# Running sums of a chunked scan: one product per head on the full array, against rows made once and spread by products over 32 rows

## The reference, cut to what matters

```python
A = adt.reshape(bsz, nc, SSD_CHUNK, SSD_GROUPS, SSD_HEADS_PER_GROUP).transpose(0, 3, 4, 1, 2)
A_cs = jnp.cumsum(A, axis=-1)
seg = A_cs[..., :, None] - A_cs[..., None, :]
Lmat = jnp.exp(jnp.where(tril, seg, -jnp.inf))
CB = jnp.einsum('bclgn,bcsgn->bcgls', Cc, Bc)
y_diag = jnp.einsum('bcgls,bgecls,bcsgep->bclgep', CB, Lmat, X)
```

## Time and profile before

| what | value |
|---|---|
| time, median of 3 runs | 3142.99 us (3139.17 to 3147.56) |
| span of the profiled execution | 3139.9 us |
| TensorE busy | 2900.7 us, 92% |
| VectorE busy | 1044.5 us, 33% |
| ScalarE busy | 569.5 us, 18% |
| mean granted TensorE clock | 0.966 |

### The profile page before, as it was taken

The page is one execution under the profiler, slowest core; times in us unless marked ns, Lnnn a source line. Parts: engine busy times, 40 slices in busy tenths (PEclk is TensorE's granted clock), DMA queues, the critical chain, the costliest instruction groups (busy, mean ns, idle before and its releaser), DMA issues. The chain is left out here.

```text
span 3139.9 us, 34204 instructions
## 1 busy us (share of the span) xinstructions
PE 2900.7 (92%) x14022; PEld 1723.2 (55%) x14022; DVE 1044.5 (33%) x2724; ACT 569.5 (18%) x1272; POOL 205.5 (7%) x369
## 2 busy tenths in 40 slices
PE   7999999999999999999999799999959997898985
PEld 4577647854567647865576455454424564343332
DVE  3444423413443523522464422121131253111112
ACT  1232311101221412102253100000010241000001
POOL 0000230000000000000000000000022020000001
PEclk9999999999999999999999899999979998999998
DMA  5357476343346437342311299999963215999996
GB/s 203 134 168 259 153 222 241 112 147 136 134 141 249 176 110 260 127 164 64 107 55 36 100 415 426 426 426 428 427 255 89 85 50 233 427 429 427 428 427 279
DMA packets 183286, 720.05 MB, mean 229 GB/s; under 512 B 16049, under 2 KB 25233, under 8 KB 158033
## 3 DMA queue, kind: packets, MB, share of 16 engines
q1 hardware_dynamic: 163600, 667.51, 54.3%
q0 software_dynamic: 19232, 50.24, 5.0%
q10 hardware_dynamic: 288, 0.01, 0.0%
HBM read 694.02 MB, written 25.53 MB: 229 GB/s over the span
## 5 line engine op out<-in xcount | busy, mean ns | idle before, releaser
L2429 PE MATMUL bank<-wslot,xgT 128*64 128x512 f32 x1040 | 488.2, 626 | 71.7 <-DMA wslot<-in_moe_w_up 68.3
L2430 PE MATMUL bank<-wslot,xgT 128*64 128x512 f32 x1040 | 488.7, 627 | 0.0
L554 PE MATMUL bank<-h1T,wslot 128*128 128x256 f32 x2176 | 476.4, 381 | 2.3 <-issue 2.2
L554 PEld LDWEIGHTS bank<-h1T,wslot 128*128 128x128 f32 x2176 | 413.1, 191 | 61.8 <-issue 6.0
L2429 PEld LDWEIGHTS bank<-wslot,xgT 128*64 128x64 f32 x1040 | 144.4, 143 | 336.5 <-issue 336.5
L2446 DVE TENSOR_TENSOR hid<-gs,bank 64x512 f32<-64x512 f32 x65 | 67.8, 1043 | 519.2 <-ACT gs L2440 519.2
L2484 PE MATMUL bank<-wslot,aT 128*64 128x512 f32 x1040 | 230.4, 595 | 1.5 <-DVE aT L643 1.5
L2404 PEld LDWEIGHTS bank<-sel,hT 128*128 128x128 f32 x1600 | 186.8, 197 | 39.5 <-issue 25.1
L2404 PE MATMUL bank<-sel,hT 128*128 128x128 f32 x1600 | 193.0, 282 | 14.1 <-DVE sel L2383 14.1
L2430 PEld LDWEIGHTS bank<-wslot,xgT 128*64 128x64 f32 x1040 | 144.4, 143 | 34.3 <-issue 34.3
L2484 PEld LDWEIGHTS bank<-wslot,aT 128*64 128x64 f32 x1040 | 73.0, 137 | 135.0 <-issue 131.3
(11 more groups left out here) (388 smaller groups left out, 3526.3 us busy)
## 6 DMA issues: line engine op xcount, KB each, us to landing
wslot<-in_moe_w_gate SPq DMA_DIRECT2D x65, 2048.0 KB, 16.1
wslot<-in_moe_w_up SPq DMA_DIRECT2D x65, 2048.0 KB, 12.3
wslot<-in_moe_w_down SPq DMA_DIRECT2D x65, 2048.0 KB, 13.2
wslot<-in_w_in SPq DMA_DIRECT2D x36, 2048.0 KB, 8.9
wslot<-in_w_ada SPq DMA_DIRECT2D x24, 2048.0 KB, 8.1
wslot<-in_ffn_w_up SPq DMA_DIRECT2D x20, 2048.0 KB, 9.1
y_rows<-yo POOLq DMA_DIRECT2D x130, 128.0 KB, 7.7
wslot<-in_w_proj_ssd SPq DMA_DIRECT2D x8, 2048.0 KB, 9.3
```

The lines of the kernel that those rows point to most:

```text
L554: ins = pe.matmul(b.t[:, 0:width], w[:, k, j * P:(j + 1) * P], xT(k), start=(k == 0), stop=(k == kc - 1))
L2429: pe.matmul(bk.t[other, :], xt.t[:, k, mine], wg[:, k, :], start=(k == 0), stop=(k == KD - 1))
L2430: ins = pe.matmul(bk.t[mine, :], xt.t[:, k, mine], wu[:, k, :], start=(k == 0), stop=(k == KD - 1))
```

## The change

`sums` makes the running sums a second time, as rows: four products with `ADT` as weights (32 columns, one column group of the array each) and `upto` as moving operand, so that the 32 heads stand on partitions 0 to 31, and again on 32 to 63, 64 to 95 and 96 to 127. VectorE copies them to a new tile `sumT`. In `chunk`, the eight products contract over 32 rows: weights one column of the identity broadcast to 128 columns, moving operand a block of 32 rows of `sumT`. Four products that follow each other lie on four row groups and write four banks, two heads a bank. All four banks are taken at once and waited for at once, VectorE adds the mask in four operations of 128x256, and one mark behind all eight products releases the first of these. The loan of a bank keeps the order of the turn: `lend` takes the bank whose turn it is, `back` puts it at the end of the list after bringing `n` below the length.

```diff
+    def lend(self):
+        at = self.n % len(self.bufs)
+        b = self.bufs.pop(at)
+        self.n = at
+        return b
+
+    def back(self, b):
+        self.n %= len(self.bufs)
+        self.bufs.append(b)
...
-        held = K.banks.bufs.pop()
+        held = K.banks.lend()
...
+        sumT = K.sb("sumT", [P, TT, P], ctx=ctx)
...
                 pe.matmul(b.t[:, 0:SHEADS], K.c("upto"), d(ADT), start=True, stop=True)
+                for i in range(P // SHEADS):
+                    pe.matmul(b.t[SHEADS * i:SHEADS * (i + 1), P:2 * P], d(ADT), K.c("upto"), start=True, stop=True)
...
+                K.dve.mark(v.tensor_copy(sumT[:, t, :], b.t[:, P:2 * P]).then_inc(K.dve.sem, 1))
...
-        K.banks.bufs.append(held)
+        K.banks.back(held)
...
-                for q, hs in enumerate(heads):
-                    bq = K.banks.next()
...
-                        for due in K.due(pe, *small, *bq.free):
...
-                            ins = pe.matmul(bq.t[:, i * P:(i + 1) * P],
-                                            dts[:, t, ADT, h:h + 1].broadcast_to([P, P]), K.c("upto"),
-                                            start=True, stop=True)
+                rows4 = P // SHEADS
+                bqs, exps = [K.banks.next() for _ in range(rows4)], []
...
+                    for due in K.due(pe, *small, *[m for bq in bqs for m in bq.free]):
+                        pe.wait_ge(*due)
+                    for j in range(2):
+                        for i, bq in enumerate(bqs):
+                            at, h = SHEADS * i, HPG * g + 2 * i + j
+                            ins = pe.matmul(bq.t[:, j * P:(j + 1) * P],
+                                            K.ident[at:at + SHEADS, at + h:at + h + 1].broadcast_to([SHEADS, P]),
+                                            sumT[at:at + SHEADS, t, :], start=True, stop=True)
+                    K.mp = K.pe.mark(ins.then_inc(K.pe.sem, 1))
+                spread = K.mp
+                for i, bq in enumerate(bqs):
...
-                            dc.t[:, 4 * q:4 * q + 4, :], bq.t[:, :].rearrange("p (h l) -> p h l", h=4),
-                            K.c("segmask").unsqueeze(1).broadcast_to([P, 4, P]), ALU.add).then_inc(K.dve.sem, 1))
+                            dc.t[:, 2 * i:2 * i + 2, :], bq.t[:, 0:2 * P].rearrange("p (h l) -> p h l", h=2),
+                            K.c("segmask").unsqueeze(1).broadcast_to([P, 2, P]), ALU.add).then_inc(K.dve.sem, 1))
```

More of the change, by code:

```diff
@@ L1374, in chunk @@
                 dc = decay.next()
-                heads = [[HPG * g + 4 * q + i for i in range(4)] for q in range(HPG // 4)]
-                exps = []
-                for q, hs in enumerate(heads):
-                    bq = K.banks.next()
-                    @block.tensor
-                    def _(pe):
-                        for due in K.due(pe, *small, *bq.free):
-                            pe.wait_ge(*due)
-                        for i, h in enumerate(hs):
-                            ins = pe.matmul(bq.t[:, i * P:(i + 1) * P],
-                                            dts[:, t, ADT, h:h + 1].broadcast_to([P, P]), K.c("upto"),
-                                            start=True, stop=True)
-                        K.mp = K.pe.mark(ins.then_inc(K.pe.sem, 1))
+                rows4 = P // SHEADS
@@ new lines, in chunk, with _ @@
+                bqs, exps = [K.banks.next() for _ in range(rows4)], []
+                @block.tensor
+                def _(pe):
+                    for due in K.due(pe, *small, *[m for bq in bqs for m in bq.free]):
[7 more added lines that the diff above has]
+                    K.mp = K.pe.mark(ins.then_inc(K.pe.sem, 1))
@@ L1390, in _ @@
+                spread = K.mp
+                for i, bq in enumerate(bqs):
                     @block.vector
                     def _(v):
-                        for due in K.due(v, K.mp, *dc.free):
+                        for due in K.due(v, spread, *dc.free):
                             v.wait_ge(*due)
                         K.mv = K.dve.mark(v.tensor_tensor(
-                            dc.t[:, 4 * q:4 * q + 4, :], bq.t[:, :].rearrange("p (h l) -> p h l", h=4),
-                            K.c("segmask").unsqueeze(1).broadcast_to([P, 4, P]), ALU.add).then_inc(K.dve.sem, 1))
+                            dc.t[:, 2 * i:2 * i + 2, :], bq.t[:, 0:2 * P].rearrange("p (h l) -> p h l", h=2),
+                            K.c("segmask").unsqueeze(1).broadcast_to([P, 2, P]), ALU.add).then_inc(K.dve.sem, 1))
@@ L1402, in _ @@
                             act.wait_ge(*due)
-                        for i, h in enumerate(hs):
-                            K.ml = K.act.mark(act.activation(dc.t[:, 4 * q + i, :], dc.t[:, 4 * q + i, :], ACT.Exp,
+                        for j in range(2):
+                            h = HPG * g + 2 * i + j
+                            K.ml = K.act.mark(act.activation(dc.t[:, 2 * i + j, :], dc.t[:, 2 * i + j, :], ACT.Exp,
                                                              bias=dts[:, t, NCS, h:h + 1]).then_inc(K.act.sem, 1))
@@ L1407, in chunk @@
                 yield
-                for q, hs in enumerate(heads):
+                for q in range(2):
                     @block.vector
                     def _(v):
-                        for due in K.due(v, exps[q], cm):
+                        for due in K.due(v, exps[2 * q + 1], cm):
                             v.wait_ge(*due)
@@ L2627, in route @@
         late, dif, incl = self.kept
-        logits = K.banks.bufs.pop()
+        logits = K.banks.lend()
         logits_free = logits.free
@@ L2741, in route @@
         chosen = K.mv
-        K.banks.bufs.append(logits)
+        K.banks.back(logits)
         b = K.banks.next()
```

## The result

The changed kernel takes 3160.54 us (median of seven runs, 3146.25 to 3162.06); the kernel before, on the same chip, 3141.41 us (seven runs, 3139.17 to 3147.56). These two also ran at a higher mean granted clock, 0.967 and 0.966, where the other five have 0.962 to 0.965. The forecast was 3144.0 us with a range from 3135 to 3151. The profiled execution took 3161.46 us for a span of 3159.6, 19.7 us more than the span in the earlier trace rows.

A forecast was written before the change was run, and what follows sets the result against it. TensorE was taken to set the scan's pace, with VectorE, which empties the banks, behind. Bank order -6.0, sums +1.0, banks +0.9 and clock +5.1 gave +1.0 us on the median 3142.99: 3144.0 us, range 3135 to 3151.

The forecast's parts named there:

- Spreading on four row groups: Scan: a chunk's spreading products take 0.75 instead of 1.79 us, 16.6 us less in all if nothing else holds TensorE.
- The banks: Scan: second chunks wait about 2 us for four banks, released by VectorE's mask; no gain from faster products, +0.9 us.
- The clock: Behind eight new scan waits of about 2.0 us: three falls to half clock at 1.7 us each, +5.1 us.
- The sums: In `sums`: four more products of 32 columns a chunk, 0.5 us in a layer, +1.0 us.
- The order of the banks: Layer 2 before its sums: the held bank comes seventh or eighth, so the 6.30 us wait shrinks, -6.0 us.
- The clock falls at nearly every new wait: Rival, scan: eight falls at 1.7 us, +13.6, in all +9.5 us, 3152.5 us; chance 0.10 for six to eight falls.
- row groups don't take turns: Denies the rival that row groups in the scan take turns, a chunk costing 2.09 us: +6.6, 3149.6 us, chance 0.06.
- the order does act: Denies the rival that the bank order changes nothing in layer 2: +7.0, 3150.0 us, chance 0.04.
- the gain doesn't come: Denies the rival that the scan's gain comes in full, second chunk finding banks free: -21.6, 3121.4 us, chance 0.05.

The follow-up runs named there:

- the filled version: Changed kernel with eight more of CB's products, results overwritten, before the second chunk's own: 3140.87 us, ratio 1.0002 to the kernel before.
- the two versions that differ in them alone: Kernel before with the new bank order, 3133.66 us; the same with the rows also made and copied in `sums` but not read, 3140.89 us.
- the order alone: Kernel before with only the new order of banks (`lend` and `back`): 3133.66 us, ratio 0.9975.
- full products: Changed kernel with spreading products over 128 rows again, rows unread: 3151.65 us; with its second chunk also waiting for the first chunk's last mask: 3165.42 us.
- half the filling: Changed kernel with four extra CB products, not eight, before the second chunk's own: 3143.42 us, ratio 1.0005 to the kernel before.

## Why the prediction was wrong

- **Spreading on four row groups**: right. 0.73 us for sixteen instructions, 0.66 to the next line; 0.75 was taken. One sentence beside it is off: a speedup of 4 by itself would give 16 x (1.79 - 0.45) = 21.4 us; the 16.6 hold 0.3 us of borders a chunk.
- **The banks**: right, in place and size. The waits are 2.06 and 1.95 us against "2.05" and "about 2". That the state product is late by exactly the 0.16 us forecast is in part luck: the products start 3.52 us behind the first CB, not 3.43, and take 0.66 us, not 0.75. Up to L1442, before any fall, the first two stretches are 0.32 and 0.31 us late, where 0.23 was forecast. This is where the 16.6 us went. That TensorE stands for VectorE's mask is shown by the filled version: 2 us of other work before it move nothing. Of what the Trainium skill says against the change ("TensorEngine Tiling (Array Packing)"), PSUM Bottleneck is borne out by the eight waits. Gotcha 1, a bank for each row tile, is what the kernel was built by; no run here tests it.
- **The clock** is the step that failed: three falls at 1.7 us were taken, +5.1, and six came that cost 22.2 us, 3.7 on average. The count was off by a factor of two, the price by another; either alone would have left the sum at 3149 to 3150 us, inside the range. The count came from eleven waits, four of which, all in the experts, had ended in a fall; in the scan it was six of eight, with the same length of wait. The price came from one fall with 1.7 us lost. That was the usual size in the trace of before: 23 of its 29 pieces lost 1.7 us, two lost 3.4 (around 58 to 65.5 and 891 to 898), and four lasted 27 to 34 us (in the one from 1754.7 on TensorE was busy for 13.8 of 30.7 us). So more rows of that trace would have widened the bound, but not given 3.7 us; that pieces behind the scan's waits run to 6.8 and 13.7 us only the traces made afterwards show. The range ended at 3151, below even the rival with eight falls, 3152.5.
- **The sums**: +1.0 taken, +1.1 by the spans, but 7.2 by the medians of the two versions that differ in them alone. In the changed kernel's own trace layer 1 has +1.9, of which 1.7 are a fall behind the wait of 1.65 us before them. The rows aren't what it hangs on: it stands also in the trace of the order alone, which has no rows, and not in that of the filled version, which has them. As instructions they were priced rightly; what the medians have on top comes with a lower mean clock.
- **The order of the banks**: -6.0 taken; -7.1 by the order alone, and -4.3 in the changed kernel's trace, with the rows' 0.5 and a fall at 897.5 us in it. Right in sign, and near in size.
- **The rivals**: row groups don't take turns, the order does act, the gain doesn't come. "The clock falls at nearly every new wait" was the nearest, at a chance of 0.10 and with half the price: at 3.7 us for each of six falls its formula gives -6.0 + 1.0 + 0.9 + 22.2 = +18.1, and 19.7 was measured by the spans, 19.1 by the medians.

**What stays open.** Which of two equal waits the clock falls behind, and for how long. Two executions of the changed kernel share one pattern, two others were faster, and the same wait of 1.65 or 1.91 us has a fall behind it in one trace and none in another. Among the pieces behind bank waits of the scan, the ones of 6.8 and 13.7 us stand only in versions with products of 32 rows, but outside the scan the trace of before has two of 6.8 us without them, and no run here says by what a piece becomes long.

## What to carry to other kernels

Before TensorE's work is made shorter, count the banks back from each request: where the release is set by VectorE, the time saved turns into standing. And standing is not neutral: here eight waits of 2.0 us, 16 us that were hidden behind VectorE, brought 22.2 us of lost clock, so that a gain that is "hidden anyway" can end as a loss. When falls are priced from a trace, take all that it holds, and leave the range open upwards where none of them stands in the same surroundings. And prefer the form that asks for no more banks than before (two groups on two banks, 1.16 us) over the one with the fastest products (four on four, 0.73).

## What the runs showed of the hardware that was not expected

- Waits of 1.95 to 2.06 us came with half clock in six of eight places (changed kernel), waits of 1.9 to 2.0 us in seven of eight (full products); waits of 1.05 to 1.17 us in two of eight (half the filling), waits of 1.0 to 1.1 us in none of eight (full products).
- Once fallen in the scan, the clock stayed at half for 3.4, 6.8 or 13.7 us though TensorE was busy for most of it (13.60 of 14.00 us in the window at 1034).
- Work whose result is thrown away, eight products of CB's shape before each second chunk, took 19.7 us off the changed kernel's median.
- From the start of a chunk's sixteen instructions to the next line it took 1.79 us on the full array, 1.09 on two row groups and 0.66 on four, borders included: each doubling divides the time by about 1.6, not by 2.
